# The mixer recurrence of a two-block model on one core: the order of work inside a chunk step, and a longer load ring for the modulation weights

## The reference, cut to what matters

```python
m_lat = jnp.split((c_lat_act @ w_ada[i] + b_ada[i])[:, None, :], 6, axis=-1)
m_ctx = jnp.split(c_ctx_act @ w_ada[i] + b_ada[i], 6, axis=-1)
...
def _rwkv7_scan(s0, r, w, k, v, a, b):
    def step(S, inp):
        r_t, w_t, k_t, v_t, a_t, b_t = inp
        sa = jnp.einsum('bhvk,bhk->bhv', S, a_t)
        S = S * w_t[:, :, None, :] + sa[..., None] * b_t[:, :, None, :] + v_t[..., None] * k_t[:, :, None, :]
        return S, jnp.einsum('bhvk,bhk->bhv', S, r_t)
...
k_dir = _heads((k[:, :, None, :] * (1 + (iclr - 1) * rw_k_a)).astype(f32), RW_HEADS)
rw_args = [(rh, dh[:, :, d], k_dir[:, :, d], vh, -kk, kk * ih[:, :, d]) for d in range(2)]
bonus = (bonus_f + bonus_b) * vh
```

## Time and profile before

| | us |
|---|---|
| median of 3 runs | 3222.06 (3222.06 to 3226.5) |
| profiled execution, its own time | 3222.01 |
| its span, first to last instruction | 3220.1 |
| end of CTX preparation (first scores) | 350.2 |
| CTX chunk steps | 350.2 to 481.9 |
| LAT preparation | 481.9 to 549.0 |
| LAT chunk steps | 549.0 to 684.3 |

### The profile page before, as it was taken

How to read it: one execution, slowest core, us unless ns; L and a number is a source line. 1 busy time by engine, 2 the same in 40 slices (tenths; PEclk the granted TensorE clock), 3 DMA queues, 4 the chain that set the end, 5 groups by cost and what they waited for, 6 DMA issues and landing times.

```text
span 3220.1 us, 66623 instructions
## 1 busy us (share of the span) xinstructions
PE 3020.7 (94%) x27360; PEld 2255.0 (70%) x27360; DVE 1941.0 (60%) x3608; ACT 1424.9 (44%) x2294; POOL 8.0 (0%) x17
## 2 busy tenths in 40 slices
PE   5998797989999989889999999999999999999998
PEld 3866694976888876743333333369988999998998
DVE  3768767664333243666666666666685666667566
ACT  3334223223222143556666666654457344445543
POOL 0000000000000000000000000000000000000000
PEclk8998897999999999989999999999999999999999
DMA  5232306012232242259999999955543555543454
GB/s 212 96 129 92 131 4 229 4 34 79 92 98 92 97 146 72 94 219 377 384 378 379 389 378 404 372 206 184 181 131 105 189 182 170 182 157 119 147 180 156
DMA packets 123298, 585.25 MB, mean 182 GB/s; under 512 B 13440, under 2 KB 17024, under 8 KB 88896
## 3 DMA queue, kind: packets, MB, share of 16 engines
q1 hardware_dynamic: 122544, 575.57, 49.3%
q0 software_dynamic: 528, 6.43, 0.5%
HBM read 580.89 MB, written 1.05 MB: 181 GB/s over the span
## 4 chain that ended last, share of the span: by engine, by line
PE 83%; DVE 9%; ACT 3%; DMA 2%; issue 1%; SPq 1%; DVEq 0%; ACTq 0%
PE ps L2408 21%; PE ps L311 16%; PE ps L312 16%; PE ps L313 16%; DMA ada_late<-wada 1%; PE ps L1743 1%; PE ps L1732 1%; PE ps L828 1%; PE ps L1740 1%; DVE w_lo L274 1%; PE ps L2419 1%; PE ps L752 1%; DVE mxv L2122 1%; ACT w_hi L270 0%; DMA w_raw<-wstream 0%
## 5 line engine op out<-in xcount | busy, mean ns | idle before, releaser
L274 DVE TENSOR_TENSOR w_lo<-w_raw,w_hi 128x1024 fp32r<-128x1024 f32 x463 | 565.6, 1224 | 596.4 <-ACT w_hi L270 592.4
L311 PE MATMUL ps<-a_hi,w_hi 128*128 128x256 f32 (+1 forms) x2660 | 838.5, 315 | 47.0 <-DVE a_lo L771 19.1
L312 PE MATMUL ps<-a_lo,w_hi 128*128 128x256 f32 (+1 forms) x2660 | 837.0, 315 | 0.0
L313 PE MATMUL ps<-a_hi,w_lo 128*128 128x256 f32 (+1 forms) x2660 | 833.5, 313 | 0.0
L270 ACT ACTIVATE w_hi<-w_raw 128x1024 fp32r<-128x1024 f32 x463 | 487.5, 1055 | 573.8 <-PE ps L313 526.2
L311 PEld LDWEIGHTS ps<-a_hi,w_hi 128*128 128x128 f32 x2660 | 509.9, 192 | 88.7 <-issue 44.1
L2590 DVE COPY wx<-wset 128x512 f32 x1188 | 424.7, 421 | 224.5 <-PE ps L2408 204.2
L2530 ACT ACTIVATE wx<-wset 128x512 f32 x792 | 444.1, 621 | 217.1 <-PE ps L2408 203.4
L312 PEld LDWEIGHTS ps<-a_lo,w_hi 128*128 128x128 f32 x2660 | 506.3, 190 | 30.8 <-issue 0.5
L313 PEld LDWEIGHTS ps<-a_hi,w_lo 128*128 128x128 f32 x2660 | 505.8, 190 | 31.1
L2408 PE MATMUL ps<-wx,xT 128*32 128x512 f32 x2640 | 378.4, 597 | 5.2 <-DVE wx L2590 5.2
(11 more groups left out here) (522 smaller groups left out, 3736.9 us busy)
## 6 DMA issues: line engine op xcount, KB each, us to landing
wset<-wexp SPq DMA_DIRECT2D x264, 1024.0 KB, 7.8
w_raw<-wstream SPq DMA_DIRECT2D x463, 512.0 KB, 3.3
ada_late<-wada SPq DMA_DIRECT2D x80, 512.0 KB, 6.3
ada_raw<-wada SPq DMA_DIRECT2D x16, 512.0 KB, 9.0
bia<-bias POOLq DMA_DIRECT2D x1, 4096.0 KB, 13.7
con<-consts SPq DMA_DIRECT2D x1, 1824.0 KB, 16.0
conb<-constsb POOLq DMA_DIRECT2D x1, 1224.0 KB, 6.1
hT<-ctxT SPq DMA_DIRECT2D x1, 1024.0 KB, 12.8
```

The lines of the kernel that those rows point to most:

```text
L274: nc.vector.tensor_tensor(wlo[:, slot, :], raw[:, slot, :], whi[:, slot, :].bitcast(F32), ALU.subtract).then_inc(lo_ready.sem, 1)
L311: nc.tensor.matmul(out, lhs[0], rhs[0], start=start, stop=False, skip_group_check=skip)
L312: nc.tensor.matmul(out, lhs[0], rhs[1], start=False, stop=False, skip_group_check=skip)
L313: return nc.tensor.matmul(out, lhs[1], rhs[0], start=False, stop=stop, skip_group_check=skip)
```

## The change

- The load ring has 12 tiles, three quads, on three semaphores. The third quad lies over `hT`, which is therefore loaded again behind the last modulation tile; VectorE waits for that (`h_in` 64) before the residual sum.
- In the preparation one operation writes `ar[..., 0, :]` for all four m, and one writes `(ic - 1) * ka` for all four. `rw_prep` is raised once for each direction, and TensorE waits for it direction by direction.
- In a chunk step the four operations `br`, `nl`, `tt[:, d, 0]` (two) come first for each direction and release it; the two operations of `tt[:, d, 1]` follow for both directions with a signal of their own (`t1_in`), which TensorE now waits for in level 0 too. `kr` is made during the last level, and the right side waits for it (`kr_in`). The bonus operation comes behind the levels.
- v is transposed once in each segment, at n = 0, in two halves of two chunks, to a tile `vts` that all four steps read.
- The product of L1740 goes to the second half of banks 4 and 5 in place of banks 2 and 3, which now hold the key scores until the last level.

```diff
-ADA_RING = 8
+ADA_RING = 12
...
             sp.wait_ge(S("ada_used").sem, ADA_LATE // 4)
+            sp.dma_start(hT[:, :, 0:SEG], io["ctxT"]).then_inc(*S("h_in").dma)
+            sp.dma_start(hT[:, :, SEG:T2], io["xT"]).then_inc(*S("h_in").dma)
...
-                             ).then_inc(*deep_loaded[4 + t // 4 % 2].dma)
+                             ).then_inc(*deep_loaded[3 + t // 4 % 3].dma)
...
+                link(nc.vector.scalar_tensor_tensor(
+                    ar[:, d, :, :, 0, :].rearrange("p m c l -> p (m c) l"), flc(kn[:]), -1.0, flc(exc[:]),
+                    ALU.mult, ALU.mult))
                 for m in range(4):
-                    link(nc.vector.scalar_tensor_tensor(
-                        ar[:, d, m, :, 0, :], c4(kn[:])[:, m], -1.0, c4(exc[:])[:, m], ALU.mult, ALU.mult))
                     link(nc.vector.tensor_tensor(ar[:, d, m, :, 1, :], c4(zr)[:, m], c4(ee[:])[:, m], ALU.mult))
...
-                for m in range(4):
-                    link(nc.vector.tensor_scalar(ic[:, m, :], ic[:, m, :], -1.0, pc("ka", m, 1), ALU.add, ALU.mult))
+                link(nc.vector.scalar_tensor_tensor(ic[:], ic[:], -1.0, bc(pc("ka").unsqueeze(2), [P, 4, SEG]),
+                                                    ALU.add, ALU.mult))
...
-            dve.sem_inc(S("rw_prep").sem, 1)
+                dve.sem_inc(S("rw_prep").sem, 1)
...
-            if n == 0:
-                pe.wait_ge(*S("rw_prep").next("pe"))
             for d in range(2):
-                if n > 0:
-                    pe.wait_ge(*S("st_done").next("pe"))
+                pe.wait_ge(*S("st_done" if n else "rw_prep").next("pe"))
...
-            pe.wait_ge(*S("tm_sb").next("pe"))
-            pairs(lambda d, m, e: nc.tensor.matmul(ps[hp(e), 6, col(m, d)], zseg(8 + m, seg, hp(e))[:, cs[d]],
+            for half in range(2 if n == 0 else 0):
+                pe.wait_ge(*S("tm_sb").next("pe"))
+                pairs(lambda c, m, e: nc.tensor.matmul(ps[hp(e), 6 + half, col(m, c)],
...
                     pe.wait_ge(*S("x_sb").next("pe"))
-                    if lv > 0:
-                        pe.wait_ge(*S("t1_in").next("pe"))
+                    pe.wait_ge(*S("t1_in").next("pe"))
...
             for d in range(2):
+                pe.wait_ge(*S("kr_in").next("pe"))
                 heads_of(d, rhs).then_inc(*S("rh_ps").one)
...
-            dve_bonus(dve, link, seg, n)
             for d in range(2):
                 dve.wait_ge(*S("n_ps").next("dve"))
...
                 link(nc.vector.tensor_tensor(br[:, d, :, :], b4(d), bc(mx[:, d, :].unsqueeze(1), [P, 4, P]), ALU.mult))
+                link(mask_n(0, d))
...
+                nc.vector.tensor_tensor(tt[:, d, 0, :, :], tt[:, d, 0, :, :], e4, ALU.add).then_inc(*S("lv_in").one)
+            for d in range(2):
                 link(nc.vector.tensor_tensor(tt[:, d, 1, :, :], br[:, d, :, 0:RC],
                                              bc(lvm[:, 1, 0, d, :].unsqueeze(1), [P, 4, RC]), ALU.mult))
-                link(nc.vector.tensor_tensor(tt[:, d, 1, :, :], tt[:, d, 1, :, :], e4, ALU.add))
-                link(nc.vector.tensor_tensor(kr[:, d, :, :], b4(2 + d), bc(mx[:, d, :].unsqueeze(1), [P, 4, P]),
-                                             ALU.mult))
-                link(mask_n(0, d))
-                dve.sem_inc(S("lv_in").sem, 1)
+                nc.vector.tensor_tensor(tt[:, d, 1, :, :], tt[:, d, 1, :, :], e4, ALU.add).then_inc(*S("t1_in").one)
             for lv in range(RLEV):
-                if lv < RLEV - 1:
-                    for d in range(2):
+                for d in range(2):
+                    if lv < RLEV - 1:
                         link(mask_n(lv + 1, d))
+                    else:
+                        nc.vector.tensor_tensor(kr[:, d, :, :], b4(2 + d), bc(mx[:, d, :].unsqueeze(1), [P, 4, P]),
+                                                ALU.mult).then_inc(*S("kr_in").one)
...
+            dve_bonus(dve, link, seg, n)
...
             dve.wait_ge(*S("mod_more").next("dve", 2))
+            dve.wait_ge(S("h_in").sem, 64)
```

More of the change, by code:

```diff
@@ L817, in sp_ada_late @@
                 sp.dma_start(ada_late[:, t % ADA_RING, :], io["wada"][ADA_EARLY + t]
-                             ).then_inc(*deep_loaded[4 + t // 4 % 2].dma)
-        DEEP_BEFORE = [64] * 4 + [ADA_LATE // 8 * 64] * 2
+                             ).then_inc(*deep_loaded[3 + t // 4 % 3].dma)
+        ADA_QUADS = ADA_LATE // 4
+        DEEP_BEFORE = [64] * 3 + [64 * (len(range(r, ADA_QUADS, 3)) + (r == 0)) for r in range(3)]
         def pe_quad(tiles, k0, bank):
@@ L1445, in build @@
         ldd, cud, icd, eed = (ld0, ld1), (cu0, cu1), (ic0, ic1), (ee0, ee1)
-        br, kr, tt, xs, nl, btt, ktt, vtt, rh, uu, _r = lay(t0_, [
+        br, kr, tt, xs, nl, btt, ktt, rh, uu, _r = lay(t0_, [
             ("br", [P, 2, 4, P]), ("kr", [P, 2, 4, P]), ("tt", [P, 2, 2, 4, RC]),
             ("xs", [P, 2, 4, RC]), ("nl", [P, 2, 2, 4, RC]), ("btt", [P, 2, 4, RC]),
-            ("ktt", [P, 2, 4, RC]), ("vtt", [P, 2, 4, RC]), ("rh", [P, 2, 4, RC]), ("uu", [P, 2, 4, RC])])
+            ("ktt", [P, 2, 4, RC]), ("rh", [P, 2, 4, RC]), ("uu", [P, 2, 4, RC])])
         assert _r <= ob
+        vts = sb("vts", [P, NRC, 4, RC], at=ob - 352 - 4096)
         def zseg(i, seg, rows=slice(0, P)):
@@ L1724, in pe_solve @@
                       ).then_inc(*S("bkv_ps").one)
-            pe.wait_ge(*S("tm_sb").next("pe"))
-            pairs(lambda d, m, e: nc.tensor.matmul(ps[hp(e), 6, col(m, d)], zseg(8 + m, seg, hp(e))[:, cs[d]],
-                                                   ident[hp(e), hp(e)], start=True, stop=True)
-                  ).then_inc(*S("bkv_ps").one)
+            for half in range(2 if n == 0 else 0):
+                pe.wait_ge(*S("tm_sb").next("pe"))
+                pairs(lambda c, m, e: nc.tensor.matmul(ps[hp(e), 6 + half, col(m, c)],
+                                                       zseg(8 + m, seg, hp(e))[:, (2 * half + c) * RC:(2 * half + c + 1) * RC],
+                                                       ident[hp(e), hp(e)], start=True, stop=True)
+                      ).then_inc(*S("bkv_ps").one)
             for lv in range(RLEV):
@@ L1746, in pe_solve @@
             pe.wait_ge(*S("tm_sb").next("pe", 2))
+            vtt = [vts[:, c, :, :] for c in ch]
             def rhs(d, m, e):
@@ L1765, in yy @@
                 nc.tensor.matmul(o, uu[hp(e), d, m, :], br[hp(e), d, m, RC:2 * RC], start=False, stop=False)
-                return nc.tensor.matmul(o, vtt[hp(e), d, m, :], kr[hp(e), d, m, RC:2 * RC], start=False, stop=True)
+                return nc.tensor.matmul(o, vtt[d][hp(e), m, :], kr[hp(e), d, m, RC:2 * RC], start=False, stop=True)
             def ss(d, m, e):
@@ L1770, in ss @@
                 nc.tensor.matmul(o, btt[hp(e), d, m, :], uu[hp(e), d, m, :], start=True, stop=False)
-                return nc.tensor.matmul(o, ktt[hp(e), d, m, :], vtt[hp(e), d, m, :], start=False, stop=True)
+                return nc.tensor.matmul(o, ktt[hp(e), d, m, :], vtt[d][hp(e), m, :], start=False, stop=True)
             for d in range(2):
@@ L1780, in act_solve @@
         def act_solve(act, n):
-            for dst, b_ in ((btt, 6), (ktt, 7), (vtt, 6)):
+            moved = [(btt[:], 6), (ktt[:], 7)]
+            if n == 0:
+                moved += [(vts[:, 0:2, :, :], 6), (vts[:, 2:4, :, :], 7)]
+            for dst, b_ in moved:
                 act.wait_ge(*S("bkv_ps").next("act"))
-                nc.scalar.activation(dst[:].rearrange("p d m l -> p (d m l)"), ps[:, b_, :], ACT.Copy
+                nc.scalar.activation(dst.rearrange("p d m l -> p (d m l)"), ps[:, b_, :], ACT.Copy
                                      ).then_inc(*S("tm_sb").one)
@@ L1829, in dve_solve @@
                         dve.wait_ge(*S("t_ps").next("dve"))
-                        nc.vector.tensor_tensor(tt[:, d, 0, :, :], tt[:, d, 0, :, :], bank(2 + d), ALU.add
+                        nc.vector.tensor_tensor(tt[:, d, 0, :, :], tt[:, d, 0, :, :], bank(4 + d, 1), ALU.add
                                                 ).then_inc(*S("lv_in").one)
```

11 lines of the change are left out of this document (5 added, 6 removed).

## The result

The kernel after the change takes 3184.91 us (median of 4 runs, 3181.43 to 3187.76), the kernel before, on the same chip, 3222.06 (4 runs): a ratio of 0.9886, with a 95% interval of 0.9871 to 0.9901. That is 37.2 us less, where 39 were forecast. The profiled execution after took 3181.43, its span is 3179.6 (before 3220.1).

What follows compares the result with a forecast made beforehand. TensorE bounds the kernel, so only its waits and low clock can be won, with VectorE's 14 operations bounding a step's start. 12.5 + 4.3 + 4.6 + 8.0 + 9.5 = 38.9 off 3222.0 gives 3183, range 3173 to 3196.

Steps and rivals of the forecast that it cites:

- steps n = 1 to 3 without the last: Five chunk steps, each 2.5 us shorter by VectorE's earlier release: 12.5, plus 4.3 for the low clock going.
- last LAT step: LAT's n = 3, where VectorE splits weights first: 4.6 us gained, half of the clock included, bounds 3.5 and 5.7.
- CTX preparation and n = 0: CTX's modulation loads and first chunk step: earlier quads, earlier release and shorter n = 0 gain 8.0 us (6.2 to 8.9).
- LAT preparation and n = 0: LAT's modulation loads and first chunk step: earlier quads and a shorter n = 0 gain 9.5 us (8 to 11).
- Clock: Three chunk steps with n > 0: low clock goes with the wait ahead of it, 4.3 us in all, at worst none.
- the forecast's margin for TensorE and ScalarE: Chunk step: VectorE still sets level 1's start; the 2.5 us gain could reach 3.0, where TensorE would set it alone.
- The failed step: Second load of `hT`, 2 MB near 540 us, some 5 us of DMA, delays nothing wanted before 640.
- First ring wait: Wait before `ssd` with one more quad queued: costs nothing if quads land in order, up to 5.1 us if not.
- the rival of shared engines: Third quad's packets mix with the awaited quad's, each landing up to 5.5 us later: about 3193, chance 0.12.
- rival of an idle ring: Preparations: ring still waits quad by quad because SyncE issues late; about 3198, chance 0.05.
- little gained per step: Chunk steps: ScalarE's copies and new waits leave only 1 us a step, low clock stays; 3197, chance 0.08.
- a lasting low clock: Short pauses hold TensorE at 1.2 GHz in over 18 of 38 levels, eating the gain; all: near 3267, chance 0.02.

Runs made afterwards that it cites:

- e6_filler: The kernel before with 64 useless matmuls put in TensorE's wait of level 0: 3215.65 us, ratio 0.9977 to the kernel before.
- e4_reload_late: The changed kernel with the three weight tiles issued first and the halves of `hT` loaded behind LAT's steps 0 and 1: 3182.94 us, ratio 0.9876.
- e12_burst_later: The changed kernel with both `hT` loads and the weight tiles, 3.5 MB, held back into LAT's n = 2: 3188.22 us, one run.
- e1_ring8: The changed kernel with the load ring of 8 tiles and without the second load of `hT`: 3196.14 us, ratio 0.9917.
- e3_tiles_first: The changed kernel with the three weight tiles issued ahead of the two `hT` loads: 3182.48 us, ratio 0.9877.
- e7_prep_ops: The changed kernel with both merges of VectorE operations in the preparation undone: 3180.94 us, one run.

## Why the prediction was right

The forecast was 3183, the result 3184.91. By the ruler, with n = 0 measured from the end of what comes before it:

| term | forecast | measured |
|---|---|---|
| steps n = 1 to 3 without the last | 12.5 + 4.3 | 19.0 |
| last LAT step | 4.6 | 6.5 |
| CTX preparation and n = 0 | 8.0 | 6.5 |
| LAT preparation and n = 0 | 9.5 | 8.25 |
| sum | 38.9 | 40.25 |

*Steps.* The mechanism holds: the wait went, and VectorE's run up to level 1 still sets the instant. A step at full clock gained 2.94, not 2.5. The forecast put every operation 0.46 behind the one before it. Those behind an operation whose only signal goes to TensorE start 0.34 apart (441.76 to 442.10, 443.81 to 444.15): level 1 stands 6.3 behind the scores instead of 6.8. That the bonus had to be moved was mistaken: moved or not, an ordinary step takes 28.8. That v's transposes lay in idle time before fits the rows (0.93 beside a wait of 2.38), but after the change they would have cost 0.62 a step, which the forecast's margin for TensorE and ScalarE didn't say.

*Clock.* 4.51 - 2.94, 4.33 - 2.94 and 4.33 - 2.93 give 4.4 for the three steps, where 4.3 was forecast, and `e6_filler` shows the cause.

*Last LAT step.* 6.5 for 4.6, beyond the upper bound of 5.7: the clock came back whole, where half was taken, about 1.1, and the shorter pitch gives the rest. The wait between the two X groups is 1.30 where 1.6 was said. That the clock came back whole is luck of this execution. Six traces have the code of this step and the wait of 1.30; in the change, `e4_reload_late` and `e12_burst_later` the step takes 30.85 to 30.87, but in `e1_ring8`, `e3_tiles_first` and `e7_prep_ops` 32.10 to 32.29, with groups at 1.2 GHz behind the wait, as in `e7_prep_ops`:

```profile
619.00 0.68 PE L1735 MATMUL ps<-tt,nl 64*64 64x64 f32 x16 [1.30 <-DVE tt L1821]
619.89 1.12 PE L1742 MATMUL ps<-xs,tt 64*64 64x64 f32 x16 [0.21 <-DVE tt L1825]
```

So half of the clock was a fair forecast of the step, and a wait of 1.30 isn't yet short enough.

*CTX preparation.* The ring did more than was forecast (first scores 342.7 for 343.4 to 345.2), 7.5 earlier. The term was too large by 1.5 all the same: direction 1 found VectorE at work until 347.0 (346.6 forecast), and behind that wait its scores ran at 1.2 GHz, 1.9 us more, so that n = 0 lost 1.0 where it was to gain 1.25. The forecast had no low clock there; that 6.5 lies above its lower end, 6.2, is two misses of opposite sign.

*LAT preparation.* First scores 56.55 behind its start, 58 to 60 forecast: better than said. The failed step is "the second load of `hT` ... nothing behind it in SyncE's queue is wanted before 640", costed at nothing. Nobody waits for its data; but beside it TensorE loses 2.84, which the argument about queues and due times couldn't see.

*First ring wait.* TensorE begins on the second quad 13.82 behind SyncE's first issue (13.79 before), and its waits for the first two are 4.13 and 1.65 (4.18 and 1.51): the third quad behind them costs nothing here, and the rival of shared engines falls. By the Trainium skill's rule ("DMA: Bandwidth & Descriptors", section "Queues, rings and completion order") it could have cost; this trace shows no such loss. The rival of an idle ring falls with 19.5 us of waits for 43.8; the rivals of little gained per step and of a lasting low clock fall with steps of 28.8.

## What to carry to other kernels

Look for the one wait per repetition and count what the releasing engine does ahead of it that the waiter doesn't need yet; release after the part that it needs, then look whether the next chain is near, for it may be 0.3 away. A wait of 2.4 us on TensorE was followed here by another 1.4 to 1.6 us of low clock in three steps of five, so price both, and test the clock with filler work. A load that nobody waits for still isn't free when it fills the DMA engines beside long hand-unrolled matmul code, whose instructions come over them too: spread it over several stages.

## What was not expected of the hardware

- Beside 3.5 MB of loads at 378 to 384 GB/s TensorE pauses 0.4 to 2.5 us between two matmuls, released by nothing in the profile, and the pauses move with the load (n = 0: 2.84 in all; moved to n = 2: 2.05). At 1.5 MB there was one of 0.22, in one trace of several. Each pause ends 1.2 to 1.6 us behind the end of a 16 KB instruction packet.
- Two operations of VectorE on 256 elements that follow each other through a semaphore start 0.46 apart, two that don't 0.34, though both take 0.42: the second starts before the first one's row ends.
- In the kernel before the same wait of level 0 was followed by the low clock in three of the five ordinary steps and not in the other two (2.38 in CTX's n = 1 and in its n = 3); a wait of 0.51, with filler in the rest, in none. In the last LAT step a wait of 1.30 was followed by it in three traces of six.
